# A two-layer hybrid trunk on one core: in-chunk products of the state-space scan with the weights' role swapped, and a new order of single units around the convolution

## The reference, cut to what matters

```python
def ssd_scan(x, dt, a, b, c, h0):
    la = jnp.cumsum(dt * a, axis=2)
    xdt = x * dt[..., None]
    seg = la[:, :, :, None] - la[:, :, None]
    decay = jnp.exp(jnp.where(lower[None, None, :, :, None, None], seg, -jnp.inf))
    cb = jnp.einsum('bctgn,bcsgn->bctsg', c, b)
    y_intra = jnp.einsum('bctsg,bctsgh,bcsghp->bctghp', cb, decay, xdt)
    w_end = jnp.exp(la[:, :, -1:] - la)
    states = jnp.einsum('bcsgn,bcsgh,bcsghp->bcghpn', b, w_end, xdt)
    ...
    y_inter = jnp.einsum('bctgn,bcghpn,bctgh->bctghp', c, h_in, jnp.exp(la))
    return (y_intra + y_inter).reshape(...), h_last
```

## Time and profile before

| | |
|---|---|
| device time, median of 3 runs | 1152.93 us (1152.9 to 1155.31) |
| the profiled execution: its own time | 1153.43 us |
| its span, first to last instruction | 1151.5 us |
| granted TensorE clock, mean | 0.992 |
| TensorE busy in the span | 1105.1 us (96%) |
| VectorE, ScalarE, GpSimd busy | 593.3, 362.1, 176.5 us |

### The profile page before, as it was taken

The page is one execution under the profiler, slowest core; times in us unless marked ns, Lnnn a source line. Parts: engine busy times, 40 slices in busy tenths (PEclk is TensorE's granted clock), DMA queues, the critical chain, the costliest instruction groups (busy, mean ns, idle before and its releaser), DMA issues.

```text
span 1151.5 us, 11913 instructions
## 1 busy us (share of the span) xinstructions
PE 1105.1 (96%) x4259; PEld 593.2 (52%) x4259; DVE 593.3 (52%) x1235; ACT 362.1 (31%) x838; POOL 176.5 (15%) x168
## 2 busy tenths in 40 slices
PE   5999999899999999999999999999999999999988
PEld 1765555455554444555544444444455555556654
DVE  0456566576746376666410216511346654446776
ACT  1522112244422345444300112112234434334440
POOL 0301000098632200000000003300011210000000
PEclk9899999999999999999999999999999999999999
DMA  9914240457653101001003040222021030200001
GB/s 351 332 3 147 77 147 1 146 194 246 214 197 129 55 1 56 1 1 55 1 0 128 0 159 1 73 73 73 1 73 46 28 109 1 74 1 1 1 1 73
DMA packets 47345, 94.16 MB, mean 82 GB/s; under 512 B 2886, under 2 KB 4711, under 8 KB 47287
## 3 DMA queue, kind: packets, MB, share of 16 engines
q1 hardware_dynamic: 43701, 84.56, 21.0%
q10 hardware_dynamic: 3330, 8.67, 2.0%
q0 software_dynamic: 256, 0.18, 0.4%
HBM read 91.17 MB, written 2.23 MB: 81 GB/s over the span
## 4 chain that ended last, share of the span: by engine, by line
PE 90%; DVE 4%; SPq 2%; DMA 1%; ACT 1%; issue 1%; POOL 0%; DVEq 0%; ACTq 0%; POOLq 0%
PE ps L741 48%; PE ps L1004 10%; PE ps L932 7%; PE ps L1040 4%; PE ps L1062 4%; PE ps L904 3%; PE ps L951 2%; PE ps L916 2%; PE ps L983 2%; PE ps L1052 2%; PE ps L973 2%; PE ps L758 2%; DVE pool_mem L1199 1%; DMA xs_all<-in_x_dram 1%; PE ps L783 1%
## 5 line engine op out<-in xcount | busy, mean ns | idle before, releaser
L741 PE MATMUL ps<-ring,hT 128*128 128x512 f32 x736 | 320.5, 593 | 1.0 <-DVE hT L1183 1.0
L741 PEld LDWEIGHTS ps<-ring,hT 128*128 128x128 f32 x736 | 138.0, 190 | 165.4 <-issue 164.2
L741 PE MATMUL ps<-hT,ring 128*128 128x512 f32 (+1 forms) x512 | 172.2, 495 | 7.9 <-DVE pool_mem L1199 7.9
L741 PEld LDWEIGHTS ps<-hT,ring 128*128 128x128 f32 x512 | 98.6, 195 | 75.1 <-issue 67.6
L1821 POOL TENSOR_SCALAR stat<-stat 128x8 f32<-128x8 f32 (+3 forms) x52 | 20.4, 392 | 752.9 <-DVE stat L1379 237.5
L932 PE MATMUL ps<-ring,hT 128*128 128x512 f32 x192 | 88.9, 594 | 0.8 <-DVE pool_mem L1434 0.8
L1411 DVE TENSOR_REDUCE stat<-ps 128x1 f32<-128x768 f32 x64 | 60.9, 952 | 52.4 <-PE ps L1040 52.2
L1004 PE MATMUL ps<-ring,hT 128*128 128x512 f32 x192 | 85.7, 593 | 1.6 <-DMA ring<-in_ev_w_out_dram 1.6
L1478 DVE TENSOR_TENSOR pool_mem<-ps,pool_mem 128x512 f32<-128x512 f32 x36 | 24.8, 688 | 92.1 <-PE ps L1004 87.0
L1822 POOL TENSOR_TENSOR stat<-stat 128x8 f32<-128x8 f32 (+3 forms) x52 | 66.1, 1271 | 4.3
L1199 DVE SCALAR_TENSOR_TENSOR pool_mem<-ps,halftap,pool_mem 128x254 f32<-128x254 f32 (+3 forms) x96 | 59.1, 616 | 3.4
(11 more groups left out here) (202 smaller groups left out, 1439.2 us busy)
## 6 DMA issues: line engine op xcount, KB each, us to landing
ring<-in_mod_w_dram SPq DMA_DIRECT2D x10, 2048.0 KB, 8.0
ring<-in_od_w_in_dram SPq DMA_DIRECT2D x8, 2048.0 KB, 8.0
ring<-in_ev_w_in_dram SPq DMA_DIRECT2D x7, 2048.0 KB, 9.0
pool_mem<-la_rows_dram SPq DMA_DIRECT2D x24, 512.0 KB, 6.6
ring<-in_ev_w_out_dram SPq DMA_DIRECT2D x4, 1536.0 KB, 6.5
ring<-in_od_w_out_dram SPq DMA_DIRECT2D x2, 2048.0 KB, 8.0
ring<-in_mod_w_dram ACTq DMA_DIRECT2D x1, 2048.0 KB, 9.1
pool_mem<-in_mod_w_dram SPq DMA_DIRECT2D x1, 2048.0 KB, 20.4
```

What stands on the lines that cost most here:

```text
L741: mm = pe.matmul(bank[:, 0:width], lhs_of(k), rhs_of(k), start=(k == 0), stop=(k == count - 1))
```

## The change

1. **`intra`.** The 64 columns of x become the weights and the 128 x 128 matrix the moving operand; two heads go to the two column halves of the array (outputs in partitions 0 to 63 and 64 to 127). ScalarE copies the 128 x 256 result to `yT_q`, and a new stage `yback` turns it back with two transposes a quad. The result banks are 5 and 6; bank 3 alone takes what is turned back.
2. **`ysum`** waits for `yback`; both stand a step later, behind `hcd` of the next step.
3. **`sel`** reads its triangle from SBUF (`gt`) where it read a copy in bank 6.
4. **Start.** `modpick` replaces the `modsum` of layer 0's first four slabs and `modcol`'s transposes: four products with 2 moving columns per slab, straight into columns in bank 6. Two tiles of tokens are loaded ahead of the `kvdt` slab.
5. **Convolution.** `dt`, `mod`, `modsum` and `diag` stand between `xbc f 1` and `xbc f 0`.
6. **Banks** are given in the order in which parts stand, passing over those held by a unit cut in parts.
7. **`ynorm`, `ytr`** stand ahead of parts 1, 2 and 3 of the next `z` (of parts 1, 3 and 5 of an `out0`).
8. **`out0`'s last slab** is loaded when the slab in its place was last read, not at the end of that unit.
9. In layer 1 one product moves from the last head's step to behind it.

```diff
@@ stages_layer0 @@
-    st += [("mod", 0, 0), ("mod", 0, 1), ("modsum", 0, 0), ("mod", 0, 2), ("modsum", 0, 1), ("mod", 0, 3)]
-    st += [("modsum", 0, 2), ("modsum", 0, 3), ("modcol", 0), ("norm", 0, 0), ("norm", 0, 1), ("trt", 0)]
+    st += [("mod", 0, 0), ("mod", 0, 1), ("modpick", 0), ("mod", 0, 2), ("modpick", 1), ("mod", 0, 3)]
+    st += [("modpick", 2), ("modpick", 3), ("modcol", 0), ("norm", 0, 0), ("norm", 0, 1), ("trt", 0)]
...
-        st += [("xbc", f, 1), ("xbc", f, 0)]
-        if n >= 1 and conv_order[n - 1] not in (10, 11):
-            st.append(("xtr", conv_order[n - 1]))
+        st.append(("xbc", f, 1))
...
+        if 5 <= n < 5 + NT:
+            st.append(("diag", n - 5))
+        st.append(("xbc", f, 0))
+        if n >= 1 and conv_order[n - 1] not in (10, 11):
+            st.append(("xtr", conv_order[n - 1]))
...
         st.append(("hcd", d, c))
+        if i >= 1:
+            st += [("yback", n - 2) for n in quads] + [("ysum",) + STEPS[i - 1]]
...
-        st.append(("ysum", d, c))
...
-            parts[1].append(late.pop(0))
-            parts[3] += late
-            late = []
+            for j in range(1, 4):
+                parts[j].insert(0, late.pop(0))
@@ banks @@
+        if bank[m] is None:
+            bank[m] = min((b for b in range(3 if m in THREE_BANKS else 2) if b not in held), key=lambda b: last[b])
...
+            last[bank[m]] = n
+            held.add(bank[m])
+        if s == u:
+            held.remove(bank[m])
@@ sync @@
+            for t in range(2):
+                load_tile(t)
             load_slab(SLAB_NO[("kvdt",)])
...
+                if stage == HALF_READ:
+                    sp.wait_ge(half_read, 1)
+                    load_slab(HALF_SLAB)
@@ tensor @@
+                elif kind == "modpick":
+                    wait_done(pe, ("mod", 0) + a)
+                    for j in range(4):
+                        col = 2 * (4 * a[0] + j)
+                        mm = pe.matmul(ps[:, 6, col:col + 2], mod_part0[:, a[0] % 2, j * P:(j + 1) * P], pick,
+                                       start=(col == 0), stop=True, skip_group_check=True)
...
-                    if step >= 2:
-                        pe.wait_ge(ysum_done, step - 1)
+                    if n >= 2:
+                        pe.wait_ge(yt_copied, n - 1)
                     pe.wait_ge(em_ready, n + 1)
-                    for i in range(4):
-                        h = 4 * q + i
-                        mm = pe.matmul(ps[:, 3 + 2 * (step % 2), (h % 8) * HD:(h % 8 + 1) * HD], emat[:, n % 4, 0, i, :],
-                                       xs[:, c, h * HD:(h + 1) * HD], start=True, stop=True)
+                    for j in range(2):
+                        for u in range(2):
+                            h = 4 * q + 2 * j + u
+                            mm = pe.matmul(ps[u * HD:(u + 1) * HD, 5 + n % 2, j * P:(j + 1) * P],
+                                           xs[:, c, h * HD:(h + 1) * HD], emat[:, n % 4, 0, 2 * j + u, :],
+                                           start=True, stop=True)
                     mm.then_inc(intra_ready, 1)
+                elif kind == "yback":
...
+                    if step >= 1:
+                        pe.wait_ge(ysum_done, step)
+                    pe.wait_ge(yt_copied, n + 1)
+                    for j in range(2):
+                        col = (2 * (n % 2) + j) * P
+                        mm = pe.transpose(ps[:, 3, col:col + P], yT_q[:, n % 2, j * P:(j + 1) * P], ident)
+                    mm.then_inc(yback_ready, 1)
@@ vector @@
-                        link(V.tensor_copy(ps[:, 6, 0:P], gt))
...
-                    after = ps[:, 6, 0:P].bitcast(mybir.dt.int32).unsqueeze(1).to_broadcast([P, 4, P])
+                    after = gt.bitcast(mybir.dt.int32).unsqueeze(1).to_broadcast([P, 4, P])
...
-                    dve.wait_ge(intra_ready, 2 * step + 2)
+                    dve.wait_ge(yback_ready, 2 * step + 2)
@@ scalar @@
+                elif kind == "intra":
+                    n = a[0]
+                    act.wait_ge(intra_ready, n + 1)
+                    if n >= 2:
+                        act.wait_ge(yback_ready, n - 1)
+                    A.copy(yT_q[:, n % 2, :], ps[:, 5 + n % 2, 0:2 * P]).then_inc(yt_copied, 1)
```

108 lines of the change are left out of this document (60 added, 48 removed).

## The result

The changed kernel takes 1173.99 us (median of 4, 1172.62 to 1174.12) against 1153.29 for the kernel before on the same chip: ratio 1.0174, 95% interval 1.0159 to 1.0189. The forecast was 1173.1, slower. The profiled execution took 1172.62, with a span of 1170.8.

What follows compares the result with a forecast made beforehand. TensorE, working 96% of the span, was taken as the bound. From 1153.4: start −2.0, convolution +3.5 and +1.9, scan +12.5, attention +3.5 and +1.9, half slab −1.6 give 1173.1 us; 8-in-10 range 1157 to 1186.

Steps and rivals of the forecast that it cites:

- the lock: Scan: `sel` with two SBUF inputs and GpSimd's instructions exclude each other whole; up to +17 us, chance 0.58.
- circle: Scan: yadd, `ex` pair, `sel`, `inter`, `emul`, `hcd`, `ysum` wait in a ring, 9.6 to 9.7 us a round; alone about +1.
- Start: Kernel start: with the tile loaded ahead of the `kvdt` slab, ScalarE's Square starts at 27.92, not 29.92; −2.0 us.
- Convolution waits: Convolution: four 512-column products wait for their banks until VectorE's taps end, 11.4 us against 7.9; +3.5.
- Clock: Convolution: waits near 2 us may drop TensorE's clock for the next product; one more fall taken, +1.9 us.
- Scan: Scan: the lock's middle value, +12.5 us, between +7.5 if VectorE always goes first and +17.4.
- the +17.4: Scan, upper end: six rounds pay 12.2 us, four others 11.0, 11.0, 9.7 and 9.1; last yadd starts at 353.4.
- Attention: Attention with z: four waits of about 1.95 us for the first `ytr`'s bank, +3.5, and one clock fall, +1.9.
- (a): Rival, scan: `sel` stays free of GpSimd, so the scan gives +1; 1161.6 us, chance 0.24.
- (b): Rival, scan: a circle round costs under 9.1 us, TensorE stays the bound and the clock holds; 1148.2 us, chance 0.12.
- (c): Rival: units fill the convolution and attention waits, with taps ending 3 us sooner; 1127.5 us, chance 0.04.
- (d): Rival, scan: column halves don't run side by side, `intra` 0.9 a quad, adding 6 us of TensorE work; chance 0.02.

Runs made afterwards that it cites:

- the first experiment: Changed kernel with `sel` reading its triangle from PSUM again, both quads' `intra` in bank 5, one 512-column ScalarE copy a step: 1162.03 us, ratio 1.0068.

## Why the forecast was right, step by step

The mechanism that decided the time, the lock at `sel` in a circle of yadd, `sel` and `ysum`, is the one that the runs show. That the total came within 1 us is in part luck: the errors of the terms, from −1.4 to +2.2, cancel.

**Start, −2.0.** Measured −2.66 at the first `xbc`; the transposes begin at 30.94, 1.96 earlier, and the first `kvdt` product ran in 4.12 instead of 4.80 us. But the reason given was half a reason. The working took ScalarE as free at 27.92 and blamed the transfer; in the kernel before, two `modsum` copies held it until 29.7. The figure held because the change removed these too. And −2.66 is one profile's figure. Among the eleven profiles of kernels with this start the first `xbc` begins between 61.3 and 63.6. In the two earliest, of which the changed kernel's 61.5 is one, the product for the last mod slab took 1.9 us, as in the kernel before; in the other nine it took 2.6 to 3.6, in part or whole at the lower clock.

**Convolution waits, +3.5.** Measured 11.2 against 7.9; each of the four waits came within 0.2 of the stated one. The terms as written fit less well: +8.9 less +6.4, +5.5 and +5.0, with 0.1 of hand-over, gives 2.6, 2.6, 3.5 and 4.0, not 2.2, 2.1, 3.0 and 3.8. Counted from the end of the product, the short taps ended at +8.4 to +8.6, and TensorE came at +6.3, +6.6, +5.7 and +5.2. **Clock, +1.9**: one fall more, as chosen; nothing in the working could have told three from two or four, and three of the six profiles with this order have two.

**Scan, +12.5 between 7.5 and 17.4.** Measured +14.7. The middle was taken because nothing told which engine goes first. Per round it was nearly right: it stands for 10.8 a round, and ten rounds of yadd, from 243.36 to 352.41, are 10.9 each. In nine of the ten a GpSimd instruction slips in between the halves of `sel`, which then take 1.5 and 2.4 us. Five rounds last 11.7 to 12.1, two last 10.7 because their yadd is the half one of 1.3 us, and three 8.8 to 10.5. Of the 2.2 that the middle was low, 0.7 are the rounds, 0.5 the first yadd (240 and the 2.9 of the later start make 242.9), and 1.1 the end, which lies 1.9 behind the last of these yadds and not 0.8; 0.9 of that is `yback`'s wait for ScalarE's copy, a term that the working did not have. "About 0.45" a quad for `intra` was 0.51 (1.02 from one start to the next for two), `yback` 0.22 to 0.27. The sign "before `inter` and `state` of together 10 us or more" failed: those waits are 6.7, and 12.0 only with those at `intra`, `modsum` and `yback`. The six full and four shorter rounds of the +17.4 add up to 354.0 and not 353.4.

**Attention, +3.5 and clock +1.9.** The step that failed in part: the waits at `ytr` were 1.45, 1.46 and three of 1.73, not about 1.95, so +2.3; no clock fall followed them; and gaps of up to 0.3 at probabilities' transposes and products, which the working did not have, made up 1.7. The total of 4.0 against 5.4 is nearer than its parts. By its own terms (four waits of 1.95 for four of 1.06, less 0.5) the working would also have had 8.9, not 9.3.

**Half slab, −1.6**: −1.8. **Layer 1, 0**: −0.1.

Of the rivals, (a) was what the first experiment built, 1162.0 against its 1161.6; the total is nearer than its parts here too, for the scan is +2.8 and not +1. (b) is out: a round with the circle cost 10.0 where it needed under 9.1, and even without lock and circle the scan did not get shorter than before. (c) is out, but not its premise: the waits can all vanish, only not in the order that the change chose. (d) is out, with 0.51 a quad.

## What to carry to other kernels

Before an operand moves from PSUM to SBUF, look whether its instruction then has two SBUF inputs and stands beside GpSimd's work: here that was 12 us in two orders of the same work, and 4 in a third. Moving an addition "one step later" off TensorE's path can close a circle through another engine whose order was not changed; add the circle up, it needs only durations. And a unit placed in a gap takes a bank as well as time: the same four kinds of units cost 11 us of waits in one order and none in another that also kept the third bank longer, and durations from one trace were enough to choose it.
